# Projection token tiles moved into the levels of a RWKV scan, on one core of a hybrid encoder layer with a mixture of experts

## The reference, cut to what matters

```python
proj = jnp.einsum('bsd,dp->bsp', x, w_in[l])
pg, pr, pm = jnp.split(proj, [G_PROJ, G_PROJ + R_PROJ], axis=-1)
y_g = gmlp_mixer(pg, ...)       # gelu, norm, 128x128 mixing of positions
y_r = rwkv7_mixer(pr, ...)      # 6 heads of 64, two directions, a scan:
#   sa = state @ a ; state = state*w + sa*b + v*k ; out = state @ r
y_m = mlstm_mixer(pm, ...)      # 6 heads of 64, chunks of 128, gates of exp
groups = jnp.concatenate([y_g, y_r, y_m], axis=-1)
x = _layer_norm(DEEPNORM_ALPHA * x + groups @ w_out[l], ln1_g[l], ln1_b[l])
ffn = _moe(x, router_w[l], ..., exp_w2[l], exp_b2[l])   # 32 experts, top 4
x = _layer_norm(DEEPNORM_ALPHA * x + ffn, ln2_g[l], ln2_b[l])
```

## Time and profile before

| what | us |
| --- | --- |
| median of 3 runs | 1183.63 (1183.06 to 1185.85) |
| span of the profiled execution | 1184.3 |
| PE busy, weight loads busy | 1132.2 (96%), 493.9 (42%) |
| VectorE, ScalarE, GpSimd busy | 284.8, 221.9, 33.7 |
| first product of pair 0, 1, 2 | 111.80, 150.84, 188.25 |
| end of pair 2 | 226.70 |

### The profile page before, as it was taken

The page is one execution under the profiler, slowest core; times in us unless marked ns, Lnnn a source line. Parts: engine busy times, 40 slices in busy tenths (PEclk is TensorE's granted clock), DMA queues, the critical chain, the costliest instruction groups (busy, mean ns, idle before and its releaser), DMA issues.

```text
span 1184.3 us, 14440 instructions
## 1 busy us (share of the span) xinstructions
PE 1132.2 (96%) x5708; PEld 493.9 (42%) x5708; DVE 284.8 (24%) x738; ACT 221.9 (19%) x519; POOL 33.7 (3%) x70
## 2 busy tenths in 40 slices
PE   7999999999999999999999999999999999999997
PEld 6875778753333333333333333333333333333332
DVE  1368666662111111111111111111111111111112
ACT  1245655412111111111111111111111111111102
POOL 1000222100000000000000000000000000000000
PEclk9999999999999999999999999999999999999999
DMA  8525202599999999999999999999999999999995
GB/s 336 196 81 198 108 1 78 195 343 390 428 427 429 427 427 428 427 428 428 429 428 427 429 428 429 428 428 429 429 429 428 428 429 429 428 428 428 429 423 217
DMA packets 35649, 430.95 MB, mean 364 GB/s; under 512 B 4086, under 2 KB 4262, under 8 KB 8860
## 3 DMA queue, kind: packets, MB, share of 16 engines
q1 hardware_dynamic: 34364, 428.27, 86.2%
q0 software_dynamic: 528, 1.02, 0.3%
q10 hardware_dynamic: 720, 1.15, 0.3%
HBM read 429.37 MB, written 1.06 MB: 363 GB/s over the span
## 4 chain that ended last, share of the span: by engine, by line
PE 73%; DMA 21%; ACT 3%; DVE 2%; issue 1%; POOLq 0%; SPq 0%; POOL 0%; ACTq 0%; DVEq 0%
PE bank L1484 25%; PE bank L1503 16%; DMA ring<-in_exp_w 14%; DMA pool<-in_exp_w 7%; PE bank L1063 5%; PE bank L1456 4%; PE bank L1440 4%; PE bank L1073 3%; PE bank L1363 2%; PE bank L1468 2%; PE bank L1535 2%; ACT pool L967 1%; PE bank L1238 1%; PE bank L1253 1%; PE bank L1245 1%; PE bank L1528 1%
## 5 line engine op out<-in xcount | busy, mean ns | idle before, releaser
L1484 PE MATMUL bank<-ring,pool 128*64 128x512 f32 x1200 | 265.4, 593 | 10.9 <-DMA ring<-in_exp_w 10.9
L1484 PE MATMUL bank<-pool 128*64 128x512 f32 x848 | 188.4, 594 | 7.1 <-DMA pool<-in_exp_w 7.1
L1484 PEld LDWEIGHTS bank<-ring,pool 128*64 128x64 f32 x1200 | 85.2, 137 | 186.5 <-issue 162.4
L1503 PE MATMUL bank<-ring,pool 128*64 128x512 f32 x620 | 137.7, 595 | 3.8 <-ACT pool L967 3.8
L2191 DVE TENSOR_SCALAR pool<-pool 128x128 f32<-128x128 f32 x64 | 19.4, 346 | 474.1 <-PE bank L1484 474.1
L1484 PEld LDWEIGHTS bank<-pool 128*64 128x64 f32 x848 | 59.9, 137 | 130.6 <-issue 115.2
L942 ACT ACTIVATE pool<-pool 128x512 f32<-128x512 f32 x32 | 20.2, 631 | 416.8 <-DVE pool L2203 416.8
L1503 PE MATMUL bank<-pool 128*64 128x512 f32 x404 | 90.1, 595 | 2.7 <-ACT pool L967 2.7
L2203 DVE TENSOR_SCALAR pool<-bank 128x512 f32<-128x512 f32 x32 | 22.2, 693 | 258.1 <-PE bank L1484 258.1
L1503 PEld LDWEIGHTS bank<-ring,pool 128*64 128x64 f32 x620 | 42.9, 137 | 85.0 <-issue 77.6
L1063 PE MATMUL bank<-pool,ring 128*128 128x256 f32 x272 | 62.1, 391 | 7.0 <-DMA ring<-in_w_in_C 7.0
(11 more groups left out here) (311 smaller groups left out, 903.1 us busy)
## 6 DMA issues: line engine op xcount, KB each, us to landing
ring<-in_exp_w SPq DMA_DIRECT2D x110, 2048.0 KB, 31.9
pool<-in_exp_w SPq DMA_DIRECT2D x73, 2048.0 KB, 34.7
pool<-in_exp_w SPq DMA_DIRECT2D x9, 1024.0 KB, 8.1
ring<-in_exp_w SPq DMA_DIRECT2D x6, 1024.0 KB, 38.4
ring<-in_w_out SPq DMA_DIRECT2D x2, 2048.0 KB, 7.6
ring<-in_w_in_A SPq DMA_DIRECT2D x1, 2048.0 KB, 13.3
ring<-in_w_in_B SPq DMA_DIRECT2D x1, 2048.0 KB, 7.7
ring<-in_w_in_D SPq DMA_DIRECT2D x1, 2048.0 KB, 13.4
```

The lines of the kernel that those rows point to most:

```text
L1484: last = mm(bank[4 + g][hp, :], lhs, row(k % 2)[:, o:o + 512], start=False, stop=(k == KD - 1), skip_group_check=(k < 2))
L1503: last = mm(bank[b][SLOTS * hf:SLOTS * hf + SLOTS, :], hidden[:, k % 4, SLOTS * (k // 4):SLOTS * (k // 4) + SLOTS], w[:, 512 * hf:512 * hf ...
```

## The change

- **Order of the token tiles.** G, H, F in place of F, G, H. They are no longer ahead of the scan but cut into slices of 2 to 4 steps of k, by the table `FILL`: key (pair, level, place), value (tile, first and last step). Place 0 is ahead of a level's updates, place 1 behind them; level `NL` (7) is the first step with the states. G and H lie in pair 0, F in pair 1, all in banks 3 and 7.
- **Channel tiles 15 and 16** stand in level 1 of pair 0.
- **Operands early.** Pair 0's decay scan and relative decays come ahead of the shift of tile 11, its keys ahead of that of tile 13, its operands behind it, and the shift of tile 14 behind those. Pairs 1 and 2 are prepared in the levels of pair 0. The temporaries are written in place.
- **Gates.** The transposes of the gate columns are at level 4 of pair 0, their biases at level 5, sums at 6, maxima behind. `first_row` is gone; all six rows go through DRAM. The gate columns and the bonus sums of pairs 0 and 1 are one block at level 1 of pair 1.
- **Heads.** Heads 0 to 2 with pair 1, 3 to 5 with pair 2, none with pair 0. The output of the second mLSTM pair moves behind the last pair.
- **Gelu and sigmoids.** The gMLP's inputs and the output gates are copied out of their banks as they are; one gelu over both tiles at the start of pair 1 and one sigmoid at the start of pair 2 follow, each with its table loads.
- **SyncE.** G is loaded after channel tile 14, H after the last one, then the rows, `x` by tokens, load 0, and both halves of `w_out`.

Three places in the engines' orders follow. An entry is line, operation, output and inputs by kind of place, shape, how many in a row, and the semaphores that it waits for.

PE between channel tile 14 and the scan, before: L1109 are the transposes of v, L1063 channel tiles 15 and 16, L1116 the gate products, L1073 the first token tile.

The diff, cut to its core:

```diff
-          "E": (M0 + 512, 256, 0), "F": (M0 + 768, 384, 1), "G": (M0 + 1152, 408, 0), "H": (0, 512, 1)}
+          "E": (M0 + 512, 256, 0), "F": (M0 + 768, 384, 1), "G": (M0 + 1152, 408, 5), "H": (0, 512, 0)}
 
 
 
 OUT_ORDER = ((0, 1), (5, 6), (2, 3), (7, 4))
-TOK_TILES = [(p, c) for p in "FGH" for c in range(NCH)]
+TOK_TILES = [(p, c) for p in "GHF" for c in range(NCH)]
+TOK_BANK = (3, 7, 3, 7, 7, 7)
+
+
+
+FILL = {(0, 2, 0): ((0, 0, 4),), (0, 2, 1): ((0, 4, 8),), (0, 3, 0): ((1, 0, 4),), (0, 3, 1): ((1, 4, 8),),
+        (0, 5, 0): ((2, 0, 3),), (0, 5, 1): ((2, 3, 6),), (0, 6, 0): ((2, 6, 8),),
+        (0, 6, 1): ((3, 0, 3),), (0, NL, 0): ((3, 3, 6),), (0, NL, 1): ((3, 6, 8),),
+        (1, 1, 0): ((4, 0, 3),), (1, 1, 1): ((4, 3, 6),), (1, 2, 0): ((4, 6, 8),), (1, 2, 1): ((5, 0, 2),),
+        (1, 3, 0): ((5, 2, 4),), (1, 3, 1): ((5, 4, 6),), (1, 4, 0): ((5, 6, 8),)}
...
                     A(gd, gd, ACT.Sigmoid).then_inc(s_lora, 1)
             z_sigmoids(0)
             z_sigmoids(1)
+            key_scales(0)
             base_of(11)
             base_of(12)
             z_sigmoids(2)
             nc.scalar.preload_act_table_set("natural_log_exp_and_others")
-            base_of(13)
-            base_of(14)
+            decay_exps(0)
             act.wait_ge(s_kmx, 2)
             A(kk, kk, ACT.Ln).then_inc(s_ach, 1)
             act.wait_ge(s_ach, 1)
             A(kk, kk, ACT.Exp, scale=-0.5).then_inc(s_kkd, 1)
+            base_of(13)
+            base_of(14)
...
+                    if pt == 0:
+                        if n == 1:
+                            key_scales(1)
+                            decay_exps(1)
+                            base_of(15)
+                        if n == 2:
+                            base_of(16)
+                        if n == 3:
+                            out_gates(0)
+                            silus()
+                        if n == 4:
+                            out_gates(1)
+                            key_scales(2)
+                        if n == 5:
+                            decay_exps(2)
+                        if n == 6:
+                            row_exps()
+                    else:
+                        if n == 1:
+                            if pt > 1:
+                                args(first)
+                        if n == 2:
+                            if pt == 1:
+                                token_values(4)
+                                act.wait_ge(s_gcol, 1)
+                                A(emt, emt, ACT.Exp, scale=-1.0).then_inc(s_gcev, 1)
+                            factors(first)
+                        if n == 4:
+                            if pt == 1:
+                                token_values(5)
+                            inv_root("g" if pt == 1 else "m")
+                            args(first + 1)
+                        if n == 5:
+                            inv_root("r")
+                            factors(first + 1)
...
+                if pt == 0:
+                    gate_inputs(2)
+                    gate_inputs(3)
                 act.wait_ge(s_o, pt + 1)
                 A(oT, pview(3, 0, NCH, P), ACT.Copy).then_inc(s_oTe, 1)
                 if pt < NP - 1:
                     identities()
+                if pt == 0:
+                    gelus()
+                if pt == 1:
+                    out_sigmoids()
+            inv_root("m")
...
+            def tok_rows(j, k0, k1):
                 p, c = TOK_TILES[j]
-                piece_ready(p)
-                bank_free(NT + j)
+                if k0 == 0:
+                    piece_ready(p)
+                    if j < 2:
+                        pe.wait_ge(s_shift, NT - 1 + j)
+                    else:
+                        pe.wait_ge(s_base, NT + (j - 1 if j < 4 else j))
+                        pe.wait_ge(s_grow, 1)
                 n = PIECES[p][1]
                 w = rview(PIECES[p][2], 0, KD, n)
-                for k in range(KD):
-                    last = mm(bank[(NT + j) % 4][:, 0:n], xT[:, k, P * c:P * c + P], w[:, k, :],
+                for k in range(k0, k1):
+                    last = mm(bank[TOK_BANK[j]][:, 0:n], xT[:, k, P * c:P * c + P], w[:, k, :],
                               start=(k == 0), stop=(k == KD - 1))
-                last.then_inc(s_proj, 1)
+                if k1 == KD:
+                    last.then_inc(s_proj, 1)
+
+            def token_work(pt, n, place):
+
+                for j, k0, k1 in FILL.get((pt, n, place), ()):
+                    tok_rows(j, k0, k1)
...
-            for j in range(5):
-                tok_tile(j)
-            pe.wait_ge(s_base, NT + 4)
-            pe.wait_ge(s_vev, 1)
-            for k in range(4):
-                for c in range(NCH):
-                    last = tr(bank[4 + k // 2][0:RH, S * (k % 2) + P * c:S * (k % 2) + P * c + P],
-                              gt[:, c, RH * k:RH * k + RH], ident)
-            last.then_inc(s_gtr, 1)
-            tok_tile(5)
...
+                    if n == 1 and pt == 1:
+                        scans_turned(0, 3)
+                        gate_cols()
+                        bonus_sums(0)
+                        bonus_sums(1)
+                    if n == 2 and pt == 2:
+                        scans_turned(1, 7)
                     if n == 2 and pt:
-                        scans_turned(pt - 1, 7)
-                    if n == 2 and pt == 0:
-                        pe.wait_ge(s_nqe, 4)
-                        gate_cols()
-                    if n == (3 if pt else 2):
-                        bonus_sums(pt)
-                    if n == 4:
-                        scores(2 * pt)
+                        scores(3 * pt - 3)
+                    if n == 3 and pt == 2:
+                        bonus_sums(2)
+                    if n == 5 and pt:
+                        scores(3 * pt - 2)
+                    if n == 1 and pt == 0:
+                        t_tile(NT - 2)
+                    token_work(pt, n, 0)
                     for d in range(2):
                         update(n, d)
-                    if n == 2 and pt == 0:
-                        pe.wait_ge(s_nqe, 4)
-                        first_row()
+                    if n == 1 and pt == 0:
+                        t_tile(NT - 1)
+                    if n == 4 and pt == 0:
+                        gate_rows()
+                    if n == 5 and pt:
+                        weigh(3 * pt - 3)
+                    token_work(pt, n, 1)
...
+            prep_scan(0)
+            prep_relative(0)
+            shifted(11)
+            shifted(12)
+            dve.wait_ge(s_ss, 1)
+            kkf = kk.rearrange("p a s -> p (a s)")
+            V.tensor_scalar(kkf[:, 0:512], bank[6][:, :], 1e-24, None, ALU.max).then_inc(s_kmx, 1)
+            V.tensor_scalar(kkf[:, 512:768], bank[7][:, 0:S], 1e-24, None, ALU.max).then_inc(s_kmx, 1)
+            prep_keys(0)
+            shifted(13)
+            dve.wait_ge(s_kkd, 1)
+            link(V.tensor_tensor(kk, kk, kkraw, ALU.mult))
+            prep_operands(0)
+            shifted(14)
+            prep_scan(1)
+            prep_relative(1)
...
+                    if pt == 0:
+                        if n == 1:
+                            shifted(15)
+                            prep_keys(1)
+                        if n == 2:
+                            shifted(16)
+                            prep_operands(1)
+                        if n == 3:
+                            prep_scan(2)
+                            prep_relative(2)
+                        if n == 4:
+                            silu_products()
+                        if n == 5:
+                            gate_biases()
+                            prep_keys(2)
+                        if n == 6:
+                            gate_sums()
+                    elif pt == 1:
+                        if n == 1:
+                            gate_columns()
+                            scans_out(0, 3)
+                            args(0)
+                        if n == 2:
+                            dve.wait_ge(s_gelu, 1)
+                            norm_mean("g", gv, GW)
+                            norm_mean("r", flat(orw), HD)
+                        if n == 3:
+                            weights(0)
+                            norm_var("g", gv, gsq, GW, LN_EPS)
+                        if n == 4:
+                            norm_var("r", flat(orw), sq, HD, GN_EPS)
+                            norm_b("g", gv, GW)
+                        if n == 5:
+                            norm_b("r", flat(orw), HD)
+                            link(V.tensor_tensor(gv, gv, wide(lnb[:, 0:GW], 2), ALU.mult))
+                            V.tensor_tensor(gv, gv, wide(lnb[:, GW:2 * GW], 2), ALU.add).then_inc(s_gv, 1)
+                        if n == 6:
+                            divide(0)
+                            weights(1)
+                            args(2)
```

471 lines of the change are left out of this document (229 added, 242 removed).

## The result

| | us |
| --- | --- |
| before, median | 1183.35 (1182.83 to 1185.85, 4 runs) |
| changed, median | 1197.10 (1195.97 to 1198.03, 4 runs) |
| ratio | 1.0109, 95% interval 1.0096 to 1.0123 |
| profiled execution of the changed kernel | 1195.97, span 1194.2 |

What follows compares the result with a forecast made beforehand. The weight stream was taken to bound the whole, TensorE's chain the front. Terms -40.4 + 28.0 + 13.4 + 2.9 + 0.9 gave +4.8 (unrounded +4.86), added to the median: 1188.5 us, range 1179 to 1192.5.

Steps and rivals of the forecast that it cites:

- the start at 71: Start of the scan: VectorE's queue lets it begin at 71.4 us, not 111.8, so -40.4 us.
- pair 0 with its waits: First head pair: moved work and new waits, less what old waits hide, make it 28.0 us longer, 67.1 us.
- pair 2: Third head pair: one scores, one weighing and a wait for a division make it 2.9 us longer.
- the tail's late norm: Tail: the second head pair's norm and output stand before the turn of the groups, +0.85 us.
- the shift reaches the weight stream 1:1: Weight stream: a scan ending one us earlier or later moves the last load and the end by one us.
- The sum without a fall: Whole kernel: all stage terms added, with nothing for a falling clock, +4.8 us, unrounded +4.86.
- the term for the clock: TensorE's clock: none in the sum; a rival had it fall behind new gaps, 1191 us, chance 0.15.
- the two gaps of 3 us: TensorE idle 3.1 us ahead of the scan and 2.9 at level 5; clock falls there could cost 1.7 each.
- VectorE is not the brake: Rival: several waits for VectorE in the start and pairs vanish, 8.5 us; 1180.0 us or below, chance 0.22.
- Half of the waits are not there: Rival: half of the start's idle and half of the level-5 wait vanish, 3.0 us; 1185.5 us, chance 0.25.
- the four largest that were priced by a queue: New TensorE waits: start 3.1 us, level 5 of pair 0 2.9, level 4 of pair 1 2.1, weighing 1.0.
- the first mask: Pair 0: VectorE has pair 1's decay scan and relative decay ahead of this mask, costing TensorE 0.96 us.

Runs made afterwards that it cites:

- e5: Changed kernel, nothing moved, unread products put in TensorE's idle gaps: ahead of the scan, level 5, level 4, ahead of the weighings; 1190.81 us, ratio 1.0062.
- e3: Changed kernel with no slice ahead of the updates at level 5 of pair 0; median 1194.93 us, ratio 1.0075.
- e4: Changed kernel with the edits of e1, e2 and e3 together, arguments behind the copies in pair 2 too; median 1187.21 us, ratio 1.0039.
- e1: Changed kernel with ScalarE's decay arguments behind the copies of the turned inverse at level 4 of pair 1; median 1198.28 us, ratio 1.0116.
- e2: Changed kernel with the gelu and its table loads moved from the start of pair 1 into its level 1; median 1194.87 us, ratio 1.0080.
- e12: Changed kernel with 4 unread products in one gap only, level 4 of pair 1; median 1200.77 us, ratio 1.0136.
- e9: Changed kernel with five moves in the engines' orders, gate biases one level earlier, 4 unread products ahead of the scan; median 1187.08 us, ratio 1.0008.
- e15: Changed kernel with unread products only in the two early gaps, ahead of the scan and at level 5 of pair 0; 1197.08 us, ratio 1.0109.
- e11: Kernel before with the made wait of e6 at level 4 of pair 1, its gap filled with 5 unread products; 1185.68 us, ratio 1.0011.
- e14: Changed kernel with 2 unread products only ahead of the second weighing of pairs 1 and 2; median 1194.05 us, ratio 1.0086.
- e6: Kernel before with one wait made by two dead copies on ScalarE at level 4 of pair 1; median 1186.14 us, ratio 1.0024.

## Why the prediction was wrong

Right were the side and nearly all of the steps: what bounds the front, the start at 71, pair 0 with its waits, pair 2, the tail's late norm (0.88 us ahead of the turn of the groups), and that the shift reaches the weight stream 1:1 (10.85 us at its first piece in the chain, 9.9 at the end of the span). The sum without a fall was +4.9; e5, in which the clock falls once, has +7.3, and less 1.7 for that fall +5.6.

The step that failed is the term for the clock. The sum has nothing for it: I had it as a rival with 0.15 and wrote "1.7 each: 1190.3 to 1192". The clock cost about 8 us. Both halves of that step were wrong.

- *Whether it falls.* I looked at the two gaps of 3 us. In the profiled execution these two had no fall behind them; the falls came behind a wait of 1.88 us and behind a row of small ones (1.09 and 0.78 us, and then products of 6 and 2 columns). In other runs they do come there: at the end of the start's gap (2.80 us) in e3 and e4, behind level 5's (2.88 us) in e1 and e2. These edits left those gaps as they were, so whether a fall comes at a gap differs from one profiled execution to another. The changed kernel has nine idle gaps of 0.9 us or more between 68 and 238 us, where the kernel before has none over 0.8, and I priced two. My own row had the warning: the stretch ahead of 268.10 is no gap of 3 us, its longest idle piece is 0.62.
- *How long it lasts.* I took the 1.7 us of the earlier trace rows. The fall at 148.70 costs that. The one at 172.05 costs 5.0, since the clock stays low for over 10 us, in e12 and e9 for about 14 at a time and in e1 for 17. All of these long falls begin between level 4 and the end of a pair, where TensorE has mostly products of 64 to 128 columns. The place alone doesn't decide it: behind the same wait of level 4 the fall lasted 10 us in the changed kernel and 3.4 in e15. Why the clock comes back late is open.

So +13.7 is 5 to 6 us for the waits and the moved work, and about 8 for the clock, on average over executions; 6.3 of the 8 were taken back by filling gaps alone (e5), with all of the change in place. That the sum's 4.9 comes near the first part is a sound forecast of the queues, not of the time. The rival "VectorE is not the brake" is out: the start came 0.4 us from where its queue put it. "Half of the waits are not there" is out too: the four largest that were priced by a queue (start, level 5, level 4 of pair 1, weighing) came out within 0.3 us. The smaller ones were a little longer than priced: 1.15 us for the first mask (0.96), 0.94 ahead of the outputs (0.6). One slip of addition stands in the rival on VectorE: its four parts make 8.3 us, not 8.5, which changes nothing. The rule of the Trainium skill, "TensorE: Matmul & The Clock Gate", section "What's actually happening", that the throttled state is the default which activity releases, agrees with e5 and e11: unread products in a gap keep the clock at 1.00 where the idle gap lost it.

The plain balance of the work was right as well: 42 us of work was moved into a scan whose idle time lies in pieces of 0.2 to 0.8 us, and took up 6.9 us of them by the forecast's sum, which pairs 0 and 2 bear out; the new waits cost more than that.

What stays open: why the kernel before, which has gaps up to 0.8 us at the same places of its levels, shows no fall inside its scan in its profile; whether gaps of 0.2 to 0.8 are short enough, or its more even work between them keeps the clock, no run here tells. Nor is it shown which gap brings which fall, or what filling one gap alone (e12, e14, e15) does to the others.

## What to carry to other kernels

Before work is moved into the waits of a dependent chain, count the new idle gaps of TensorE, not only their length. Falls of the clock were seen here behind gaps of 0.62 to 2.9 us, in some executions and not in others, and the price is the stretch behind, from 3.4 to 17 us at half clock. When a kernel's executions spread by several us and the mean granted clock goes with them, compare the clocks before the waits. Look for falls in the profile of the kernel before as well, since one of them can hide in the difference of a stage. The test is cheap: put unread products into the gaps and see whether time and spread fall (1197.1 to 1190.8 here, with nothing moved).

## What the runs showed of the hardware

- A gap of 2.46 us made in the kernel before lowered the granted clock to 0.66 over the 5 us behind it in the profiled execution; with the gap filled it was 1.00 there (e11).
- Falls began behind gaps as short as 0.62 us (before, 267.94) and 0.63 (e9), and none began behind the gaps of 2.80 and 2.88 us in the changed kernel's profiled execution.
- A fall among products of 128 and 256 columns was over after 3.4 us (e5, 80.0 to 83.4). Among products of mostly 64 to 128 columns one lasted 17 us (e1, 185.5 to 202.5), and another 3.4 (e6, 174.8 to 178.2).
- At the low clock a block of four scores products took 2.07 us and at the full one 1.13; updates 2.08 and 1.05.
